# Turning normalised rows with a diagonal matmul, moving the decode row to ScalarE and GpSimd, and squaring the last two tiles before their gain

## The reference

```
h = rmsnorm(x, norm_mix_pre);  z = h @ w_in
o = nsa_attend(...)            # compressed, selected and window branches
y = s5(...)                    # state-space branch, then a GLU
merged = sigmoid(g_a) * (o @ w_branch_nsa) + sigmoid(g_b) * (o_s5 @ w_branch_s5)
x = x + rmsnorm(merged @ w_out, norm_mix_post)
hm = rmsnorm(x, norm_mlp_pre)
f = square(relu(hm @ w_mlp_up)) @ w_mlp_down
y = x + rmsnorm(f, norm_mlp_post)

def rmsnorm(x, g):             # in f32, over the last axis of 1,024
    return x * rsqrt(mean(x * x) + 1e-6) * g
```

## Time and profile before

| what | value |
|---|---|
| median of 3 runs | 1363.39 us (1362.45 to 1364.57) |
| the profiled execution's own time | 1360.91 us |
| its span | 1359.1 us |
| PE busy | 1251.5 us, 92% |
| DVE busy | 828.9 us, 61% |
| ACT busy | 305.1 us, 22% |
| POOL busy | 355.7 us, 26% |
| mean granted clock of PE | 0.965 of full speed |

### The profile page before, as it was taken

One profiled execution on the slowest core, in us unless ns is written; L12 is line 12 of the kernel. 1 busy time (PEld: TensorE's weight loads), 2 busy tenths in 40 slices (PEclk: granted clock), 3 DMA queues, 4 the chain that ended last, 5 costly groups with the idle time before them and its releaser, 6 DMA issues.

```text
span 1359.1 us, 20576 instructions
## 1 busy us (share of the span) xinstructions
PE 1251.5 (92%) x7761; PEld 1017.1 (75%) x7761; DVE 828.9 (61%) x1370; ACT 305.1 (22%) x831; POOL 355.7 (26%) x422
## 2 busy tenths in 40 slices
PE   6889899999999669999999999986999999999995
PEld 5778776668887445565788888775888888888885
DVE  7779332227888477777766554657565465466445
ACT  3463311120010355565410111032000000000012
POOL 5942324312220012222111111110111112513542
PEclk9899899899999889999999999996999999999998
DMA  9223445547667333535561332330122132131101
GB/s 264 72 79 121 148 108 170 160 146 257 242 248 248 105 91 106 162 97 167 178 225 63 109 92 80 140 111 29 62 97 90 63 114 72 62 124 63 63 1 63
DMA packets 122002, 166.15 MB, mean 122 GB/s; under 512 B 36448, under 2 KB 90400, under 8 KB 117552
## 3 DMA queue, kind: packets, MB, share of 16 engines
q1 hardware_dynamic: 103408, 104.72, 24.8%
q0 software_dynamic: 8080, 50.58, 10.5%
q10 hardware_dynamic: 10416, 9.54, 2.1%
HBM read 159.34 MB, written 13.84 MB: 127 GB/s over the span
## 4 chain that ended last, share of the span: by engine, by line
PE 81%; DVE 12%; issue 3%; ACT 3%; POOL 0%; DMA 0%; DVEq 0%; ACTq 0%; PEldq 0%
PE PS L2277 44%; PE PS L1870 13%; PE PS L2041 8%; PE PS L1847 4%; PE PS L1996 2%; PE PS L2185 2%; PE PS L2153 2%; DVE small L1659 2%; PE PS L2215 1%; DVE PS L1657 1%; DVE R L1677 1%; PE PS L1979 1%; PE PS L2020 1%; DVE hT L1259 1%; PE PS L2190 1%
## 5 line engine op out<-in xcount | busy, mean ns | idle before, releaser
L1870 PE MATMUL PS<-hT,stream 128*128 128x260 f32 (+1 forms) x800 | 187.7, 395 | 6.5 <-ACT KVU L1061 4.1
L1870 PEld LDWEIGHTS PS<-hT,stream 128*128 128x128 f32 (+1 forms) x800 | 153.7, 194 | 38.4 <-issue 6.0
L2277 PE MATMUL PS<-R,stream 128*128 128x260 f32 x720 | 168.9, 383 | 2.4 <-PE PS L2277 2.4
L2277 PEld LDWEIGHTS PS<-R,stream 128*128 128x128 f32 x720 | 135.7, 190 | 25.8 <-issue 5.5
L2277 PE MATMUL PS<-R 128*128 128x260 f32 x576 | 134.3, 390 | 3.3 <-DVE R L1822 2.1
L2277 PEld LDWEIGHTS PS<-R 128*128 128x128 f32 x576 | 111.7, 194 | 22.1 <-DVE R L1822 2.5
L2041 PE MATMUL PS<-R 128*128 128x256 f32 (+1 forms) x544 | 121.9, 383 | 5.2 <-DVE R L1500 2.4
L2277 PE MATMUL PS<-R,QO 128*128 128x260 f32 x544 | 123.6, 383 | 1.4 <-DVE QO L1703 1.4
L1777 DVE TENSOR_TENSOR R<-PS,R 128x260 f32<-128x260 f32 x100 | 42.6, 426 | 129.5 <-PE PS L2277 128.8
L2041 PEld LDWEIGHTS PS<-R 128*128 128x128 f32 x544 | 102.1, 197 | 22.1 <-issue 6.1
L2277 PEld LDWEIGHTS PS<-R,QO 128*128 128x128 f32 x544 | 103.3, 190 | 17.6 <-DVE QO L1703 1.8
(11 more groups left out here) (420 smaller groups left out, 1931.2 us busy)
## 6 DMA issues: line engine op xcount, KB each, us to landing
stream<-in_cache_kv_slc SPq DMA_DIRECT2D x128, 128.0 KB
stream<-in_w_mlp_up SPq DMA_DIRECT2D x8, 2048.0 KB
stream<-in_w_mlp_down SPq DMA_DIRECT2D x8, 2048.0 KB
stream<-in_w_in SPq DMA_DIRECT2D x4, 2048.0 KB
stream<-in_state_kv_win SPq DMA_DIRECT2D x16, 512.0 KB
stream<-in_w_in SPq DMA_DIRECT2D x8, 1024.0 KB
out_kv_win_sample<-in_state_kv_win POOLq DMA_DIRECT2D x1, 8176.0 KB, 43.3
R<-in_cache_kv_slc SPq DMA_DIRECT2D x56, 128.0 KB
```

Of the source, the lines that this page charges most:

```text
L1870: ins = M(pair(u)[0:w, hf, 0:HALF], lhs[k], rhs[k][:, HALF * hf:HALF * hf + HALF], start=(k == 0), stop=(k == n - 1))
L2277: ins = M(product_of(w, i), lhs[:, k, :], rhs[:, k, :], start=(k == 0), stop=(k == nk - 1))
```

## The change

1. **Norms before a projection.** DVE no longer scales the row tile. It scales the 128x128 identity by the column of reciprocals (a diagonal, in one of two buffers `diag`/`diag2`), and PE multiplies each 128x128 block of the unscaled rows with it: an ordinary f32 matmul in place of each transpose. This holds for both such norms.
2. **Decode rows.** In the norms after a projection, the 8-row tile is no longer added by DVE. ACT multiplies it by its reciprocal root (`sample_scale`), POOL adds it to the residual (`sample_add`, after `W_OUT`'s units ahead of unit `W_UP`, and at the end), with the semaphores `ys_scaled` and `x1s_ready`. DVE's additions go from five to four in both.
3. **Squares.** For tiles 6 and 7 ACT squares as soon as PE has turned the tile, and DVE's gain product waits for the square. Tile 6 is turned inside product 7 of the unit (between the second and the third of its four steps); even tiles wait for the fourth addition of their unit only, odd ones for the fifth and POOL's.
4. **Root.** A square root of a constant stands in ACT's program in unit `W_OUT`+1.

Two unused semaphores go. The core of the diff:

```diff
-        xn = QO[:, 0:2 * D].rearrange("p (s d) -> p s d", s=2)
+        diag = QO[:, 0:2 * P].rearrange("p (s c) -> p s c", s=2)
-        xn2 = QO[:, 5 * D:7 * D].rearrange("p (s d) -> p s d", s=2)
+        diag2 = QO[:, 5 * D:5 * D + 2 * P].rearrange("p (s c) -> p s c", s=2)
...
+            def sample_add(which, y):
+                if which == 0:
+                    pool.wait_ge(x2_in, 32)
+                pool.wait_ge(ys_scaled, which + 1)
+                G(x1[0:NB, TT, :], x1[0:NB, TT, :], y, ALU.add).then_inc(x1s_ready, 1)
...
+                if w == W_UP:
+                    sample_add(0, ytm[0:NB, TT, :])
...
+            sample_add(1, yts)
...
+            def sample_scale(which, y):
+                act.wait_ge(ssq_ready, 2 * which + 2)
+                nc.scalar.activation(y, y, ACT.Copy, scale=rstd[0:NB, TT:5]).then_inc(ys_scaled, 1)
...
-                    act.wait_ge(yg_ready, done + 1)
+                    if m < KD - 2:
+                        act.wait_ge(yg_ready, done + 1)
+                    else:
+                        act.wait_ge(yt_full, done + 1)
...
+                if w == W_OUT + 1:
+                    nc.scalar.activation(pmx[:, 0:1], epsb, ACT.Sqrt)
...
                     root(TT, TT + 1, NB).then_inc(root_ready, 1)
-                    rms(x1, R[:, 0:D], lambda t: act.wait_ge(x1_ready, t + 1))
+                    sample_scale(0, ytm[0:NB, TT, :])
+                    rms(x1, R[:, 0:D], lambda t: act.wait_ge(x1_ready, t + 1) if t < TT else act.wait_ge(x1s_ready, 1))
...
-                    if make and t + 1 < len(ROWS):
+                    if make and t + 1 < TT:
...
-                    V.tensor_scalar(dst[0:r, t % 2, :], src[0:r, t, :], rstd[0:r, t:t + 1], None,
+                    V.tensor_scalar(scales[0:r, t % 2, 0:r], ident[0:r, 0:r], rstd[0:r, t:t + 1], None,
                                     ALU.mult).then_inc(xn_ready, 1)
...
-                dve.wait_ge(yt_full, KD * g + m + 1)
+                if m < KD - 2:
+                    dve.wait_ge(yt_full, KD * g + m + 1)
+                else:
+                    dve.wait_ge(yt_sq, KD * g + m + 1)
...
-            for t, r in enumerate(ROWS):
-                y = ytp[:, t, :] if t < TT else yts
-                V.scalar_tensor_tensor(x1[0:r, t, :], y, rstd[0:r, t:t + 1], x1[0:r, t, :],
+            for t in range(TT):
+                V.scalar_tensor_tensor(x1[:, t, :], ytp[:, t, :], rstd[:, t:t + 1], x1[:, t, :],
                                        ALU.mult, ALU.add).then_inc(x1_ready, 1)
...
-                        ins = tp(PS[:, 4 + v % 4, r * k:r * k + r],
-                                 src[0:r, t % 2, P * (4 * half + k):P * (4 * half + k) + P], r)
+                        ins = M(PS[:, 4 + v % 4, r * k:r * k + r],
+                                src[0:r, t, P * (4 * half + k):P * (4 * half + k) + P], scales[0:r, t % 2, 0:r],
+                                start=True, stop=True)
...
                 for k in range(nk):
+                    if k == 2:
+                        yt_backs(inside)
                     ins = M(product_of(w, i), lhs[:, k, :], rhs[:, k, :], start=(k == 0), stop=(k == nk - 1))
...
                     if m % 2 == 0:
+                        pe.wait_ge(pr_added, 5 * (YT_BASE[g] + m // 2) + 4)
+                    else:
                         pe.wait_ge(pr_added, 5 * (YT_BASE[g] + m // 2) + 5)
                         pe.wait_ge(sum_ready, YT_BASE[g] + m // 2 + 1)
...
-                product(w, 7, A22, TB[:, 2])
+                after = yt_tiles(YT_AFTER, w)
+                split = 1 if after and after[-1][1] == KD - 1 else 0
+                product(w, 7, A22, TB[:, 2], after[:split])
...
-                yt_backs(yt_tiles(YT_AFTER, w))
+                yt_backs(after[split:])
```

More of the change, by code:

```diff
@@ L306, in build @@
         tables_done = sem("tables_done")
-        out_ready = sem("out_ready")
         lag_ready = sem("lag_ready")
@@ L317, in build @@
         sa_ready = sem("sa_ready")
-        sw_read = sem("sw_read")
         kv_store = [sem(f"kv_store{i}") for i in range(4)]
@@ L369, in build @@
         x1_ready = sem("x1_ready")
+        x1s_ready = sem("x1s_ready")
+        ys_scaled = sem("ys_scaled")
         f_ready = sem("f_ready")
@@ L1225, in _ @@
                     root(TT, TT + 1, NB).then_inc(root_ready, 1)
-                    rms(x1, R[:, 0:D], lambda t: act.wait_ge(x1_ready, t + 1))
+                    sample_scale(0, ytm[0:NB, TT, :])
+                    rms(x1, R[:, 0:D], lambda t: act.wait_ge(x1_ready, t + 1) if t < TT else act.wait_ge(x1s_ready, 1))
                     act.dma_start(gain, a["norm_mlp_post"].rearrange("(o d) -> o d", o=1).to_broadcast([P, D])
                                   ).then_inc(gain_in, 16)
-            act.wait_ge(ssq_ready, 2)
+            act.wait_ge(ssq_ready, 3)
             root(0, TT, P)
             root(TT, TT + 1, NB).then_inc(root_ready, 1)
+            sample_scale(1, yts)
             for t in range(5):
-                act.wait_ge(x1_ready, 6 + t)
+                act.wait_ge(x1_ready if t < TT else x1s_ready, 5 + t if t < TT else 2)
                 if t < TT:
@@ L1251, in _, with pre_norm @@
             V.memset(epsb, EPS).then_inc(eps_ready, 1)
-            def pre_norm(first, src, dst, gains, roots, make=None):
+            def pre_norm(first, scales, gains, roots, make=None):
                 def evac(t):
@@ L1292, in _ @@
             V.tensor_scalar(ang2, ang2, 3.1415925, -3.1415925, ALU.min, ALU.max).then_inc(ang_ready, 1)
-            pre_norm(0, xtm, xn, gT[:, 0, :], 0)
+            pre_norm(0, diag, gT[:, 0, :], 0)
             dve.wait_ge(trig_ready, 1)
@@ L1720, in row_scales @@
                 V.reciprocal(rstd[:, 0:TT], ssq[:, 0:TT])
-                link(V.reciprocal(rstd[0:NB, TT:5], ssq[0:NB, TT:5]))
+                V.reciprocal(rstd[0:NB, TT:5], ssq[0:NB, TT:5]).then_inc(ssq_ready, 1)
+                dve.wait_ge(ssq_ready, 2 * which + 2)
             def add(t):
@@ L1831, in _ @@
                     dve.wait_ge(x2_in, 32)
-                    pre_norm(10, x1, xn2, gT[:, 1, :], 6, add)
+                    pre_norm(10, diag2, gT[:, 1, :], 6, add)
                     dve.wait_ge(xnt_free, 20)
@@ L1847, in tp, with norm_transposes @@
                 return nc.tensor.transpose(out, in_, ident[0:rows, 0:rows])
-            def norm_transposes(first, src):
+            def norm_transposes(first, src, scales):
                 for v0, (t, half) in enumerate(NORM_UNITS):
@@ L1887, in _ @@
             tp(PS[:, 1, 0:2 * KD], gnat, 2 * KD).then_inc(gains_full, 1)
-            norm_transposes(0, xn)
+            norm_transposes(0, xtm, diag)
             pe.wait_ge(xnt_free, 10)
@@ L2270, in wait_bank, with product @@
                     pe.wait_ge(yg_ready, KD * w + i + 1)
-            def product(w, i, lhs, rhs):
+            def product(w, i, lhs, rhs, inside=()):
                 wait_bank("p", w, i)
@@ L2293, in _ @@
                 if w == W_UP:
-                    norm_transposes(10, xn2)
+                    norm_transposes(10, x1, diag2)
                     pe.wait_ge(xnt_free, 20)
```

## The result

The changed kernel is slower by a little: 1364.78 us against 1360.79, each the median of 18 runs; paired by chip the ratio is 1.0024 [1.0012, 1.0035], or +3.3 us. Forecast was -0.7 us, with 0.63 on a difference too small to tell. The profiled execution took 1367.06 us with a span of 1364.4, against 1360.91 and 1359.1. It is one of the slowest of its kernel (they run from 1360.15 to 1367.1), while that of the kernel before lies near its median, so the spans' +5.3 overstates the difference of the medians.

The account below looks back on a forecast made before the run. PE, busy 92% of the span, was taken as the bound. Head +0.9, middle -2.0, first MLP unit 0 and tail +0.4 sum to -0.7 us: 1360.2 profiled, 1362.7 as median, eight-in-ten range 1359.2 to 1365.5.

Parts of the forecast that it names:

- own case: Whole kernel: the prediction's main case, -0.7 us, median 1362.7, range 1361.0 to 1364.8; chance 0.45.
- Two records per product: Norms on PE: an f32 product is two instructions, a transpose one; a tile costs 3.45 us low clock, 1.8 high.
- Head, +0.9: Norm before the first projection: PE becomes slower than DVE, last eviction at 20.5 against about 19.65, +0.9 us.
- Rival 1: PE doesn't bind: products cost as little as transposes, or the clock is up early; -5.2 us, 1358.2; chance 0.10.
- Middle, -2.0: Norms between w_out and the MLP: last eviction at 932.5 against 934.5, -2.0 us, with squares -0.1 and root -1.0 included.
- I charge 0.5: Middle norm: DVE's loss to sharing reads with POOL's decode-row addition, 0.5 us, bounds nothing to 1.9.
- Rival 4: Middle norm: the clock stays low throughout, PE needing 3.45 us per tile; total +3.9 us, 1367.3; chance 0.09.
- First MLP unit, 0: First MLP products after the token sums: low clock as before, no change, bounds -1.9 and +1.7 us.
- Rival 2: First MLP unit: the clock stays high into it, PE working harder ahead of it; -1.9 us more, 1360.8; chance 0.17.
- Tail, +0.4: After the last product: squares -0.9, POOL's shared reads costing DVE's additions 1.7; last store ends at 1358.3, +0.4 us.
- rival 6: Squares ahead gain nothing, as in the middle: 0.9 us more, 1363.6; counted inside the main forecast, no separate chance.
- Rival 3: Middle and tail: POOL's 8-row addition costs DVE nothing; tail -0.9, middle -2.5, total -2.5 us, 1360.9; chance 0.12.

Follow-up runs that it names:

- mid_rows: early_only with the middle norm's decode row moved to ScalarE and GpSimd in eight pieces, the tail's kept on VectorE; ratio 0.9970 to the kernel before.
- diag_only: The kernel before with only the diagonal products in both norms; ratio 1.0008, +1.1 us.
- no_rows: The changed kernel with the decode rows back on VectorE; ratio 0.9996 to the kernel before, -0.5 us.
- pool_pieces: The changed kernel with GpSimd's decode addition cut into eight instructions of 128 columns; ratio 1.0029 to the kernel before.
- early_only: The kernel before with only the squares ahead, tile 6 turned inside product 7, and the early root; ratio 0.9972, -3.7 us.
- rows_only: The kernel before with only the decode rows moved to ScalarE and GpSimd; ratio 1.0024, +3.2 us.
- late_pool: early_only with one unread 16-column GpSimd product released by the tail's second addition; ratio 0.9992 to the kernel before.

## Why the prediction was wrong

It forecast -0.7 us; the measurement gives +3.3, and the profiled execution +5.3, 0.86 of it outside the stretches of the change. That the median, 1364.78, lies inside the range named for its own case (1361.0 to 1364.8) is luck: the range stood on a median of 1363.39 for the kernel before, which came out at 1360.79 over 18 runs. By its steps:

**Two records per product: right.** 80 a norm, 80 more in the page, half the transposes' pace. Of the Trainium skill's factor of four ("TensorE: Matmul & The Clock Gate", Terms) the records show two at 128 columns: tiles took 1.8 us at the high clock (0.89 between halves), not 3.6. Transposes alone on PE raised the clock also in mid_rows (0.50 until 921, 1.00 in 922:924), where the Trainium skill, "TensorE: Matmul & The Clock Gate", Part 4, says that the high level doesn't engage for transpose mode.

**Head, +0.9: too small.** It was +1.9 (diag_only, no_rows) to +2.55. The step that failed is the decode tile's price, 0.65 to "some 1.2": 1.8 us, since a narrow product costs as much as a wide one. The low level lasted until about 15.2 instead of 14, which at half a microsecond for each is 0.6 and was inside the prediction's bounds, the diagonal took 0.29 instead of 0.23, and in this execution the chain began 0.28 later, at 10.08 instead of 9.80. Rival 1 (PE doesn't bind) fell.

**Middle, -2.0: the root right, the rest lost.** The root's -1.0 is exact. The squares' -0.1 is too small to be told. What failed is "I charge 0.5" for POOL's addition: 1.45 us, and not where DVE waits for PE but on the first diagonal, which PE waits for. I had mostly counted on it beside additions and taken it for shared bandwidth; it is exclusive use, and for an instruction with a single tile as input too. Reduction to token sum came out at 17.98 us where some 15.95 had been forecast. Of these 2.0 us pool_pieces takes off 1.45; the other 0.6 is the decode tile again, 0.6 us longer than priced. "PE then busy without gaps" failed too: DVE's evictions of tile 0 wait for PE (0.57 and 1.02 us) and hold up the fourth addition, which begins at 930.37, and PE then has a gap of 0.41 before 932.09. That added little, for pool_pieces has the same waits and PE without a gap. Rival 4 (the clock low throughout) fell: it was 1.00 from 930 on, 9.9 us behind the reduction. In the kernel before it had risen near 926, 9.3 behind, so the real products raised it no sooner than transposes.

**First MLP unit, 0.** About -0.1: of the -1.34 the squares take 1.2. Rival 2 (the clock stays high) came half true: it stayed high through the first product and fell in the pause. The pause that I named against it is the likeliest cause, as above. That the same pause is shorter when PE is slower, as in early_only, was not in my list.

**Tail, +0.4.** The squares brought -1.2 instead of -0.9 (404.2 to 403.0 above), so rival 6 fell. Against it stood 1.7 for shared reads. The wait was 3.43 - 1.28 = 2.15 us on one addition, beyond my worst case of 2.1 by a hair and a mechanism of another kind: an addition started beside POOL's and finished one addition's time after it. ACT's closing record behind the last store stands at 1363.1, in the kernel before at 1358.9, 0.2 ahead of that span's end, so the stores alone would have let this span end near 1363.4. The remaining 1.0 is a term that the prediction did not have: the core's end comes 8.3 us after POOL's last instruction, behind POOL's DRAIN. Rival 3 (POOL's addition costs DVE nothing) is what pool_pieces makes nearly true, and it shows that the gain is then eaten by that term.

**Sum.** Head +1.6 over its term, middle +2 over, tail +1.5 over (3.08 - 1.2 against 0.4), MLP unit -0.1: about +5 over -0.7, near the profiled +5.3 less 0.86. The medians say +3.3; the executions of the changed kernel spread over some 7 us (1360.15 to 1367.1), and the profiled one is among the slowest. The terms that failed are costs of the change: the narrow product, the wait for POOL's instruction, POOL's DRAIN.

**What stays open.** Why POOL's DRAIN takes 8.0 us, and whether it does behind an instruction of another kind; whether the diagonal pays in the middle norm at the high clock; what the 0.86 us ahead of the middle norm are; how the two levels of the MLP column are met in single executions, since each kernel was profiled once.

## What to carry to other kernels

Before moving work to GpSimd, look at which DVE additions and scalings will be under way beside it, charge the one that meets it the rest of GpSimd's instruction, and let GpSimd's last instruction end 8.3 us or more before the end that the stores set. Trading a DVE scaling for an ordinary f32 product instead of a transpose doubles PE's records, narrow tiles included; in the head, where PE then ran without a pause, it cost more than it saved. Unread products that hold the clock are work for PE too: check that none stands between an operand that is ready and its product. And when PE gets faster ahead of a fixed wait, read the granted clock behind that wait first: the pause that grows may cost as much as was gained.

## What was not expected of the hardware

- GpSimd's closing DRAIN ends 8.0 us after its last compute instruction in every kernel here, and the span ends 8.2 to 8.3 us after that instruction in the changed kernel, rows_only, pool_pieces and late_pool.
- DVE's additions and scalings and GpSimd's additions and products on SBUF exclude each other to the end of the one that started first: 1.74 us for a scaling of 0.29, 3.43 for an addition of 1.28, 3.39 for a POOL addition of 2.33, 1.19 for a POOL product of 16 columns. A reciprocal of one column was not held up (0.16).
- An ordinary f32 product with 8 columns takes the time of one with 128: 1.86 us for eight calls, 16 records.
